# Rotary halves swapped by 32-partition copies on ScalarE in twelve of sixteen rotations, with three steps placed elsewhere in the order

## The reference

```
def apply_rope(t, cos, sin):
    t1, t2 = jnp.split(t, 2, axis=-1)
    rot = jnp.concatenate([-t2, t1], axis=-1)
    return (t * cos + rot * sin).astype(t.dtype)

def mixer_ab(h, cos, sin, w_in, q_norm, w_uq, w_uiq, sinks, w_out):
    ...
    aq = apply_rope(aq...); ak = apply_rope(ak...)
    ya = swa_sink_attention(aq, ak, av, sinks)
    cq = rms_norm(cq, q_norm)
    bq = apply_rope(cq @ w_uq); biq = apply_rope(cq @ w_uiq)
    bk = apply_rope(bk); bik = apply_rope(bik)
    yb = dsa_attention(bq, bk, bv, biq, bik, iw)
    return jnp.concatenate([ya, yb], axis=-1) @ w_out

def mixer_c(h, cos, sin, w_in, w_out):
    q, k, v = jnp.split(h @ w_in, 3, axis=-1)
    q = apply_rope(q...); k = apply_rope(k...)
    return moba_attention(q, k, v) @ w_out
```

## Time and profile before

| what | value |
|---|---|
| median of 3 runs | 1513.03 us (1510.76 to 1518.17) |
| the profiled execution | 1513.89 us |
| its span in the trace | 1511.9 us |
| TensorE busy | 1379.5 us, 91% |
| VectorE busy | 994.9 us, 66% |
| ScalarE busy | 599.6 us, 40% |
| first mixer, from the first rotation on | about 60 to 170 us |
| second mixer, its loop with rotations | about 434 to 510 us |

### The profile page before, as it was taken

The page is one execution under the profiler, slowest core; times in us unless marked ns, Lnnn a source line. Parts: engine busy times, 40 slices in busy tenths (PEclk is TensorE's granted clock), DMA queues, the critical chain, the costliest instruction groups (busy, mean ns, idle before and its releaser), DMA issues.

```text
span 1511.9 us, 22681 instructions
## 1 busy us (share of the span) xinstructions
PE 1379.5 (91%) x8866; PEld 1194.8 (79%) x8866; DVE 994.9 (66%) x1437; ACT 599.6 (40%) x803; POOL 0.2 (0%) x4
## 2 busy tenths in 40 slices
PE   6987979999889789999969987999997899999997
PEld 1753669998778578999869986999986676899996
DVE  3667589777977667656676875765567545575554
ACT  2433343334334433433354322533345453443332
POOL 0000000000000000000000000000000000000000
PEclk9997989999999889999979998999998999999999
DMA  9743529787284335656435321455543310455540
GB/s 358 290 172 124 183 95 355 287 305 268 76 322 132 108 111 207 234 201 220 167 112 191 134 89 56 171 191 192 185 152 112 140 57 28 167 209 187 186 154 28
DMA packets 45841, 262.91 MB, mean 174 GB/s; under 512 B 5191, under 2 KB 6855, under 8 KB 21066
## 3 DMA queue, kind: packets, MB, share of 16 engines
q1 hardware_dynamic: 32672, 216.88, 39.6%
q10 hardware_dynamic: 13102, 45.09, 8.5%
HBM read 260.89 MB, written 1.05 MB: 173 GB/s over the span
## 4 chain that ended last, share of the span: by engine, by line
PE 77%; DVE 14%; ACT 4%; DMA 3%; issue 2%; SPq 0%; DVEq 0%; ACTq 0%
PE banks L523 22%; PE banks L524 21%; PE banks L525 21%; DMA A<-ada_w 3%; DVE w_lo L1571 2%; PE banks L730 2%; PE banks L1047 2%; PE banks L687 1%; ACT A L1102 1%; ACT w_hi L1086 1%; PE banks L633 1%; PE banks L828 1%; PE banks L915 1%; PE banks L669 1%; PE banks L700 1%
## 5 line engine op out<-in xcount | busy, mean ns | idle before, releaser
L1571 DVE TENSOR_TENSOR w_lo<-raw,w_hi 128x2048 fp32r<-128x2048 f32 x193 | 439.8, 2287 | 174.9 <-ACT w_hi L1086 171.7
L1086 ACT ACTIVATE w_hi<-raw 128x2048 fp32r<-128x2048 f32 x193 | 368.8, 1913 | 228.4 <-PE banks L525 217.6
L523 PE MATMUL banks<-hT_hi,w_hi 128*128 128x256 f32 x1432 | 413.3, 289 | 5.8 <-DVE hT_lo L1560 3.3
L524 PE MATMUL banks<-hT_lo,w_hi 128*128 128x256 f32 x1432 | 409.7, 286 | 0.0
L525 PE MATMUL banks<-hT_hi,w_lo 128*128 128x256 f32 x1432 | 409.5, 286 | 0.0
L523 PEld LDWEIGHTS banks<-hT_hi,w_hi 128*128 128x128 f32 x1432 | 279.4, 195 | 12.2 <-issue 7.1
L524 PEld LDWEIGHTS banks<-hT_lo,w_hi 128*128 128x128 f32 x1432 | 279.5, 195 | 3.1 <-issue 0.7
L525 PEld LDWEIGHTS banks<-hT_hi,w_lo 128*128 128x128 f32 x1432 | 279.2, 195 | 0.0
L523 PE MATMUL banks<-w_hi,R 128*128 128x512 f32 (+1 forms) x592 | 231.5, 391 | 5.5 <-DVE R L1560 3.6
L524 PE MATMUL banks<-w_lo,R 128*128 128x512 f32 (+1 forms) x592 | 229.6, 388 | 0.0
L525 PE MATMUL banks<-w_hi,R 128*128 128x512 f32 (+1 forms) x592 | 228.9, 387 | 0.0
(11 more groups left out here) (228 smaller groups left out, 1287.2 us busy)
## 6 DMA issues: line engine op xcount, KB each, us to landing
raw<-stream SPq DMA_DIRECT2D x193, 1024.0 KB, 4.9
A<-ada_w ACTq DMA_DIRECT2D x73, 512.0 KB, 5.5
A<-ada_w SPq DMA_DIRECT2D x16, 512.0 KB, 10.9
A<-ln_g ACTq DMA_DIRECT2D x4, 512.0 KB, 3.6
A<-ln_b ACTq DMA_DIRECT2D x4, 512.0 KB, 5.4
A<-ada_w SPq DMA_DIRECT2D x1, 1536.0 KB
A<-x_t SPq DMA_DIRECT2D x2, 512.0 KB, 13.3
X<-ada_w SPq DMA_DIRECT2D x1, 1024.0 KB
```

Source lines behind the costliest of these rows:

```text
L523: pe.matmul(o, lh, rh, start=start, stop=False, skip_group_check=True)
L524: pe.matmul(o, lh, rl, start=False, stop=False, skip_group_check=True)
L1086: act.activation(w_hi[:, s, :], raw[:, s, :], ACT.Copy).then_inc(hi_done, 1)
L1571: v.tensor_tensor(w_lo[:, s, :], raw[:, s, :], w_hi[:, s, :], ALU.subtract).then_inc(lo_done, 1)
```

## The change

Twelve rotations (0, 1, 5, 6, 7 and 8 to 14) lose the product with `perm`. In its place a new step `halves` has ScalarE copy the tile four times in blocks of 32 partitions, each block from the partitions of its partner: source block `at ^ 32`, target block `at`, 512 columns each, written straight to the rotation's target. VectorE then multiplies the target in place by the sines. Rotations 2, 3, 4, 15 and MLA's keep the product. Every rotation after the first now also waits for the one before it (`roped`).

Three more things move. In the first mixer VectorE's cast of unit AB + 5 goes ahead of rotation 0 and that of AB + 6 ahead of rotation 1, and rotation 7 and the cast of AB + 9 go from ahead of the first pair's maxima to behind those of pair 1 and to pair 4; the eight rounds of top-k are spread 1, 2, 2, 3 over pairs 0 to 3, where they were 2, 2, 2, 2. In the second mixer `collect` (the values of a pair) goes behind the next pair's scores, and `some` (an `ada` slice) behind the rotation.

```
+        rope_to = [step[1:] for step in STEPS if step[0] == "rope"]
+        SWAPPED = [0, 1, 5, 6, 7] + list(range(8, 15))
...
@@ ab_steps
-            s += fills(AB + 2, "T", "h", "rope", [AB_TMP])
+            s += fills(AB + 2, "T", "h", "rope", [AB_TMP]) + [("halves", 0)]
             s += [("turn2", cq, COL["ab_q"], "cq_ab", 0)] + rest(AB + 4)
-            s += fills(AB + 3, "T", "h", "rope", [AB_TMP])
+            s += fills(AB + 3, "T", "h", "rope", [AB_TMP]) + [("halves", 1)]
-            s += rope(4) + [("gate_sum", 0, 5, 6, 0, 1)] + rest(AB + 5)
+            s += [("gate_sum", 0, 5, 6, 0, 1)] + rest(AB + 5) + rope(4)
-            s += [f[0]] + rope(6) + rest(AB + 6) + [("gate_sum", 4, 2, 3), f[1]] + rope(12) + ...
-            s += rope(14) + rest(AB + 7) + [f[3]] + rope(8) + [("gate0",)]
-            s += fills(AB + 5, "T", "h", "rope", [AB_TMP]) + rope(10)
+            s += [f[0]] + rest(AB + 6) + rope(6) + [("gate_sum", 4, 2, 3), f[1]] + rope(12) + ...
+            s += rope(14) + rest(AB + 7) + [f[3], ("halves", 5)] + rope(8) + [("gate0",)]
+            s += fills(AB + 5, "T", "h", "rope", [AB_TMP]) + [("halves", 6)] + rope(10)
             s += [("index", h) for h in range(3)] + rest(AB + 8)
-            s += fills(AB + 6, "T", "h", "rope", [AB_TMP]) + rope(0)
-            s += [("index", h) for h in range(3, IDX_HEADS)] + rope(2) + rest(AB + 9)
+            s += fills(AB + 6, "T", "h", "rope", [AB_TMP]) + [("halves", 7)] + rope(0)
+            s += [("index", h) for h in range(3, IDX_HEADS)]
             for i in range(8 + DUO_LAG):
                 s += [("duo", i, 0, 8)]
+                if i == 1:
+                    s += rope(2)
                 if i < TOPK // 16:
-                    s += [("topk",)] * 2
+                    s += [("topk",)] * (1, 2, 2, 3)[i]
...
-                if i == 6:
-                    s += rest(AB + 10)
+                if i in (4, 6):
+                    s += rest(AB + 7 + i // 2)
@@ c_steps, the loop over j
-                s += (score(c) + exps(c) if c >= 0 else []) + fills(u, ...) + rest(u - 1 + SLOTS)
-                s += (spread(c) if c >= 0 else []) + [("ahead", u)] + some(1)
+                s += score(c) if c >= 0 else []
+                s += collect(c - 1) if c >= 1 else []
+                s += (exps(c) if c >= 0 else []) + fills(u, ...) + rest(u - 1 + SLOTS)
+                s += (spread(c) if c >= 0 else []) + ([("halves", 8 + j)] if j < 7 else []) + [("ahead", u)]
                 if j:
                     s += rope(j - 1)
-                s += collect(c) if c >= 0 else []
+                s += some(1)
@@ ScalarE
+                elif kind == "halves":
+                    r = a[0]
+                    tmp, _, to, w = rope_to[r]
+                    act.wait_ge(turn_f, r + 1)
+                    if r == 5:
+                        act.wait_ge(gate_used, 2)
+                    for at in range(0, P, 32):
+                        ins = act.activation(A[at:at + 32, to:to + w], A[at ^ 32:(at ^ 32) + 32, tmp + 512 * (r % 2):][:, 0:w],
+                                             ACT.Copy)
+                    ins.then_inc(shifted, 1)
@@ VectorE, kind == "rope"
+                    if r:
+                        v.wait_ge(roped, r)
+                    if r in SWAPPED:
+                        mark(v.tensor_tensor(shape(tb), shape(f), cos, ALU.mult))
+                        v.wait_ge(*halves_of(r))
+                        link(v.tensor_tensor(shape(d), shape(d), sin, ALU.mult))
+                        v.tensor_tensor(d, d, tb, ALU.add).then_inc(roped, 1)
+                        continue
```

More of the change, by code:

```diff
@@ L233, in two_block_kernel @@
         silu_ready, row_ready = sem("silu_ready"), sem("row_ready")
+        shifted = sem("shifted")
         (ld_const, ld_row, ld_gate, ld_level, ld_bias, ld_sink, ld_vec, ld_pos, ld_x, ld_gn, ld_rope2, ld_fn) = map(sem, (
@@ L312, in ab_steps @@
             s += fills(AB + 1, "N", "h", "plain", [two(A[:, AB_TOK:AB_TOK + 512])]) + rest(3)
[L313 removed]
+            s += fills(AB + 2, "T", "h", "rope", [AB_TMP]) + [("halves", 0)]
             s += [("turn2", cq, COL["ab_q"], "cq_ab", 0)] + rest(AB + 4)
[L315 removed]
+            s += fills(AB + 3, "T", "h", "rope", [AB_TMP]) + [("halves", 1)]
             rope = lambda tile: [("rope", AB_TMP, TURNED, AB_QK + 256 * tile, 512)]
[L317 removed]
+            s += [("gate_sum", 0, 5, 6, 0, 1)] + rest(AB + 5) + rope(4)
             f = fills(AB + 4, "T", "cq_ab", "rope", [AB_TMP] * 4)
[L319 to L321 removed]
+            s += [f[0]] + rest(AB + 6) + rope(6) + [("gate_sum", 4, 2, 3), f[1]] + rope(12) + [("gate_sum", 6, 4, 7), f[2]]
+            s += rope(14) + rest(AB + 7) + [f[3], ("halves", 5)] + rope(8) + [("gate0",)]
+            s += fills(AB + 5, "T", "h", "rope", [AB_TMP]) + [("halves", 6)] + rope(10)
             s += [("index", h) for h in range(3)] + rest(AB + 8)
[L323 to L324 removed]
+            s += fills(AB + 6, "T", "h", "rope", [AB_TMP]) + [("halves", 7)] + rope(0)
+            s += [("index", h) for h in range(3, IDX_HEADS)]
             for i in range(8 + DUO_LAG):
                 s += [("duo", i, 0, 8)]
+                if i == 1:
+                    s += rope(2)
                 if i < TOPK // 16:
[L328 removed]
+                    s += [("topk",)] * (1, 2, 2, 3)[i]
                 if i == TOPK // 16 - 1:
@@ L358, in c_steps @@
                 u, c = CU + 4 + j, j - 3
-                s += (score(c) + exps(c) if c >= 0 else []) + fills(u, "T", "h", "rope", [C_TMP]) + rest(u - 1 + SLOTS)
-                s += (spread(c) if c >= 0 else []) + [("ahead", u)] + some(1)
+                s += score(c) if c >= 0 else []
+                s += collect(c - 1) if c >= 1 else []
+                s += (exps(c) if c >= 0 else []) + fills(u, "T", "h", "rope", [C_TMP]) + rest(u - 1 + SLOTS)
+                s += (spread(c) if c >= 0 else []) + ([("halves", 8 + j)] if j < 7 else []) + [("ahead", u)]
                 if j:
                     s += rope(j - 1)
-                s += collect(c) if c >= 0 else []
-            s += score(5) + exps(5) + rope(7) + rest(CU + 15) + score(6) + exps(6) + spread(5) + score(7) + spread(6) + exps(7)
+                s += some(1)
+            s += score(5) + collect(4) + exps(5) + rope(7) + rest(CU + 15) + score(6) + exps(6) + spread(5) + score(7) + spread(6) + exps(7)
             s += collect(5) + spread(7) + some(1) + collect(6) + some(1) + collect(7) + [("rows", 1, 0)]
@@ L444, in two_block_kernel, with halves_of @@
         STEPS += bound(7, "final", M3 + 31, None)
+        rope_to = [step[1:] for step in STEPS if step[0] == "rope"]
+        SWAPPED = [0, 1, 5, 6, 7] + list(range(8, 15))
+        def halves_of(r):
+            return shifted, SWAPPED.index(r) + 1
         def T_unit(u0, k):
@@ L911, in _ @@
                 elif kind == "rope":
+                    if n["turn"] in SWAPPED:
+                        n["turn"] += 1
+                        continue
                     pe.wait_ge(turn_f, n["turn"] + 1)
@@ L1812, in _ @@
                     v.wait_ge(pair_ready, n["pair"])
+                    if r:
[5 more added lines that the diff above has]
+                        v.tensor_tensor(d, d, tb, ALU.add).then_inc(roped, 1)
+                        continue
                     mark(v.tensor_tensor(shape(d), shape(f), cos, ALU.mult))
-                    v.wait_ge(turn_ps, r + 1)
+                    v.wait_ge(turn_ps, r + 1 - sum(q < r for q in SWAPPED))
                     link(v.tensor_tensor(shape(tb), shape(B[2][:, 0:w]), sin, ALU.mult))
```

1 line of the change is left out of this document (removed).

## The result

The changed kernel takes 1520.3 us in the median of 8 runs (1516.56 to 1526.34), the kernel before 1512.37 (8 runs, 1510.67 to 1518.17): a ratio of 1.0065, 95% interval 1.0044 to 1.0086. It is slower by about 8 us, where the forecast said 1513.2 with an upper end of 1519.5. The profiled run took 1524.67 us, 4.4 above the median.

What follows compares the result with a forecast made beforehand. The prediction saw engine-changing waits bounding the first mixer and TensorE pacing the second mixer's loop. First mixer +4.7 us and second -4.5 us gave +0.2, a median of 1513.2 us, range 1506.5 to 1519.5.

Steps and rivals of the forecast that it cites:

- my sum: First mixer up to the mask `chosen`: +1.7 us from copies and moves, +3.0 from the clock, +4.7 in all.
- My limits of +0.9 and +7.5: The range in us given for the first mixer's total around +4.7.
- Price of a copy, 0.49 us: Each 32x512 ScalarE copy costs as much as a whole tile; four take 1.96 us, bounds 1.8 to 2.4.
- Rotation 0, +1.0: First mixer: copies ahead of the `cq` split delay it 1.96 us; fewer VectorE waits for `perm` leave +1.0 us.
- Gate row +3.0, heads +1.96 each: First mixer: copies of rotations 5, 6, 7 delay the gate row 3.0 us and index heads 0 and 3 1.96 each.
- The clock, +3.0: First mixer: two new TensorE gaps of 4 us each bring a half-clock fall costing 1.5 us; range 0 to +5.
- The moves, -5.2 from head 5 to `chosen`: First mixer: VectorE work moved later cuts the delay from 6.9 to 1.7 us, the moved work being covered at either clock.
- rival 2: First mixer: ScalarE's queue starves TensorE, so 95 to 120 us runs at half clock; +9 us more, 1522 us, chance 10%.
- Forecast -4.5: Second mixer in us: start -1.2, loop -2.8, last rotation -0.5; limits -7.4 and -1.5.
- The path that I wrote for the loop: Second mixer: copies, high cast, halves, low cast, scaling matrices, next products; iterations of 9.2 and 10.2 us by turns.
- Rival 3: Second mixer: ScalarE copies of 0.65 us or more set the loop's pace above 9.9 us; 1516.5 us, chance 17%.
- Rival 1: Both mixers: TensorE sets the pace everywhere, so removed products and waits save 13.3 us; 1499.7 us, chance 8%.

Runs made afterwards that it cites:

- ab_part: Only the first mixer changed (order and five sets of copies), the second as in the kernel before: 1525.06 us, ratio 1.0087.
- moves_only: Changed kernel's order in both mixers, but all rotations keep their product with perm and no copies are added: 1510.91 us, ratio 0.9998 against the kernel before.
- experiments 4, 9, 10: Changed kernel with one 128x512 copy per set, 1506.83 us; only second mixer changed, copies from PSUM, 1507.65 us, or onto the same partitions, 1507.26 us.
- warm_gaps: First mixer changed, second as before, plus eight unread TensorE products at each of three waits for ScalarE: 1519.25 us, ratio 1.0040 against the kernel before.
- ab_late: First mixer changed, but four of five copy sets placed later in ScalarE's queue; second as before: 1509.14 us, ratio 0.9992 against the kernel before.
- c_part: Only the second mixer changed (order and seven sets of copies), the first as in the kernel before: 1506.45 us, ratio 0.9974.

## Why the prediction was wrong

**The first mixer, where it failed.** The scores of pair 4 wait for `chosen`, the mark of my sum: forecast +4.7 us, measured +15.3 in the profiled run (101.5 - 86.2) and +12.7 in `ab_part`, whose weights came in time. The step that failed is this sum. Of the 8.0 us between forecast and `ab_part`, 4.2 are what the moves were to give back (put at -5.2, measured -1.0 in `moves_only`). Another 3.0 are the delay by the copies ahead of the gate row and of heads 2 and 5: put at 6.9, where 4.8 at the gate row and two sets of 2.57 make 9.9. The 0.8 left are the clock's, put at +3.0; that share is what remains, not a measurement. My limits of +0.9 and +7.5 did not follow from my own bounds either: four sets of 1.8 or 2.4 us and a clock term of 0 or 5 make +1.1 to +8.5. Term by term:
- *Price of a copy, 0.49 us.* It is 0.64, outside my bounds (a set 2.57 against 1.8 to 2.4). I took the start-to-start time of whole-tile copies, which overlap; quarters don't (experiments 4, 9, 10). This is 0.6 a set, and a set above 2.4 was one of my signs of being wrong.
- *Rotation 0, +1.0.* The split of `cq` moved 4.62: 2.57 for the copies, 1.9 because the high cast's weights landed late in this run (63.23 against 61.32). TensorE waits 4.62 us at 72.25 for the low cast behind the split, a wait that the sum did not have, and its clock is at 0.50 from there to about 78. In `ab_part`, where the cast started at 60.48, the wait is 2.39 us and the clock stays at 1.00 (66 to 80 us); there the copy that waits for the rotations comes 1.9 later than before (82.60 - 55.46 against 81.11 - 55.89), not 1.0. The profiled run has pair 4 2.6 us later than `ab_part`; that this is what lifts it above the median is not shown.
- *Gate row +3.0, heads +1.96 each.* Measured in `ab_part`: +4.8, then +4.6 from gate row to head 2, then +5.1 to head 5; I had 3.0, 3.5 and 3.5 with the clock's share. The gaps that I put at 4 us were right in kind (4.62 to 4.84).
- *The clock, +3.0.* Up to head 5 the two stretches took 4.6 and 5.1 us more, which is 4.6 beyond two sets of 2.57. I priced a fall after the one at 86 to 88 us, some 3 us long, but these lasted 7 us and more. The last and longest fall, 123 to 142 us in the changed kernel, cost nothing against the order alone: from head 5 to pair 4 takes 35.0 us in the changed kernel, 35.1 in `ab_part` and 35.9 in `moves_only`, where 113 to 127 us passed at half clock without any copies. Filling the gaps (experiment 5) removes also half clock that the kernel before had, so its 8.5 us (66.0 against 57.5) are not the size of this term.
- *The moves, -5.2 from head 5 to `chosen`.* Measured -1.8 in `ab_part` (35.1 against 36.9) and -1.0 in `moves_only` (35.9). I argued that all of it is VectorE's work and covered at either clock. But VectorE did not set the pace there. Ahead of the maxima of pair 2 it waited 4.15 us for TensorE at half clock before, and it still waits 2.56 us in `moves_only` and 2.22 us (at 142.58) in the changed kernel. In `warm_gaps`, with TensorE at full clock for most of that stretch, the same steps take 32.3 us.

From the gate row to pair 4, with the time at half clock summed over windows of 1 us:

| kernel | gate row to pair 4, us | of it at half clock, us |
|---|---|---|
| before | 58.1 | 17 |
| `moves_only` | 57.1 | 18 |
| `ab_part` | 66.0 | 39 |
| `warm_gaps` | 57.5 | 8 |

The mechanism of rival 2 (1522 us, 10%) is near to what happened, with a smaller effect than its 12 us for the clock and in another stretch, so that its time is close is partly luck. The clock came back between the gaps (1.00 at 100 to 104 and 114 to 120 us) and stayed down behind the last. My reason against it, the quick return after 1.77 us of idle time, was weak: one short gap says little of a wait of 4.8 us that is followed by thin work with more waits in it. Shorter ones count too: behind 1.14 us ahead of head 2 the clock stayed at 1.00, behind 2.13 us in `ab_late` it was at 0.50 for about 6 us. The Trainium skill, page "TensorE: Matmul & The Clock Gate", section "Why this matters for your kernels", which warns of idle gaps between bursts, bears more than I gave it; experiment 5 agrees, with the clock at 0.95 instead of 0.70.

**The second mixer, where the sum was right and its parts were not.** Forecast -4.5, measured -4.3 us in `c_part` (stage 162.5 against 166.8) and -4 us in the median. That the total fits is luck, since its parts miss in both directions: the start gave 2.8 instead of 1.2 (up to the first transposing products), the loop 0.4 instead of 2.8, the rest 1.1 instead of 0.5. One pair of traces gives these, and the start alone takes 74.0 to 75.9 us in the four kernels with an unchanged second mixer. The path that I wrote for the loop is the one in the trace: copies, high cast, high half, low half, low cast, matrix. It takes 10.12 us, not 9.2: the cast starts 3.3 us after the products' end instead of 2.55, mostly for the price of the copies, and from its start to the end of the next products pass 6.8 us, where I had 6.65. The wait of 1.12 us ahead of every second pair's scores, forecast at 1.2, is there. Rival 3 (the copies set the loop's pace) is thus true of the loop, with its price of 0.65 us a copy; the start of the stage gained more.

**Rival 1** (TensorE everywhere) is out as it stands, but in the second mixer it was in reach: with the copies elsewhere in the queue the loop runs at TensorE's 9.27 us (TensorE is busy for all of it; my sum had 8.97), and the kernel at 1500.6 to 1502.4.

## What to carry to other kernels

Work moved to an idle engine costs its place in that engine's queue, not its share of busy time: look for who waits behind each new instruction, and put it where the engine itself waits. Taking work from an engine just ahead of a wait gains nothing and makes the wait longer (1.14 to 2.13 us here). A gap on TensorE can cost more than its length: here one of 4.84 us was followed by 19 us at half clock. Look at all the work behind the gap, not at the shortest fall in the trace, and at the clock that this work had already: only half clock that is new is a cost of the change. Where an engine waits for another, as VectorE did here for 4.15 us, taking work from it gives little back. Price a small piece by its own duration, without overlap, unless a row shows pieces of that kind in sequence.

## What the runs showed of the hardware

- Four ScalarE copies of 32x512 fp32 one behind the other take 0.63 us each from SBUF and 0.60 from PSUM with no overlap; one of 128x512 takes 0.62 and 0.60 and the next starts 0.52 and 0.49 after its start. The shift between partitions is free (2.53 us for four without it, 2.54 with). The instruction behind a 32x512 copy starts 0.66 us after its start, also when it writes elsewhere.
- TensorE work that nobody reads shortened the kernel: some 13 us of it, partly at half clock (5.29, 3.72 and 3.72), took the ratio from 1.0087 to 1.0040.
- In these traces the granted clock stayed at 1.00 behind the gap of 1.14 us ahead of index head 2 (before), and was at 0.50 for about 3 us behind one of 1.77 ahead of the gate row (before), for about 6 behind 2.13 ahead of head 2 (`ab_late`), and for about 19 behind 4.84 ahead of head 5 (changed). The work behind them differs, so this is no rule of the length alone.
- The same weight unit lands at different times: its high cast starts between 60.0 and 63.2 us in the fourteen traces. In the seven with the first mixer as before the gate row comes 22.5 us after this cast when the cast starts 6 us or more after the mark of the table (28.8, 29.3 and 30.0), and otherwise at 28.1 or 28.2. At pair 4 these traces show no such order (85.3, 89.0 and 86.6).
